# A hybrid attention and gating layer on eight cores: normalizing out of PSUM before the gate, and a wider tie rule in the planner

## What is computed

```python
h = rmsnorm(x, norm_g)
proj = einsum('bsd,de->bse', h, w_in) + b_in               # 1024 -> 2816
q, k, v, z_a, u_s, v_s, z_s = split(proj)                  # 512,128,128,512,512,512,512
attn = banded_sink_attention(q, k, v, sinks) * silu(z_a)   # window 128, 8 heads, 2 kv heads
#   probs = exp(scores) / (sum(exp(scores)) + exp(sink)) in effect, then probs @ v
sgu = chunked_spatial_gating(gelu(u_s), gelu(v_s), ...) * silu(z_s)
x = x + einsum('bse,ed->bsd', concat([attn, sgu]), w_out) + b_out
return rmsnorm(x, final_norm_g)
```

## Time and profile before

| what | value |
| --- | --- |
| median of 3 runs | 537.83 us (537.43 to 538.85) |
| profiled execution, its own time | 538.59 us |
| its span on the slowest core (core 3) | 537.0 us |
| spans of the other cores | 531.6 to 536.5 us |
| mean granted TensorE clock, the cores | 0.984 to 0.990 |
| TensorE matmul busy | 491.4 us, 91% |
| VectorE / ScalarE / GpSimd busy | 301.6 / 319.4 / 220.8 us |

### The profile page before, as it was taken

One profiled execution on the slowest core, in us unless ns is written; L12 is line 12 of the kernel. 1 busy time (PEld: TensorE's weight loads), 2 busy tenths in 40 slices (PEclk: granted clock), 3 DMA queues, 4 the chain that ended last, 5 costly groups with the idle time before them and its releaser, 6 DMA issues.

```text
span 537.0 us, 10160 instructions; the slowest of 8 cores (531.6 to 537.0 us)
## 1 busy us (share of the span) xinstructions
PE 491.4 (91%) x3422; PEld 234.5 (44%) x3422; DVE 301.6 (56%) x434; ACT 319.4 (59%) x543; POOL 220.8 (41%) x271
## 2 busy tenths in 40 slices
PE   1899999779999999999999999999999999997983
PEld 1346444334444445444454445444544445442431
DVE  2866865444374564455655556465565456675444
ACT  4336875563677674867558474957478545367422
POOL 2001686345045515361445515471356745432501
PEclk9999999898999999999999999999999999998998
DMA  8999993940031381472234713390344013311003
GB/s 237 337 344 319 331 213 53 204 175 1 1 118 41 76 264 54 157 163 74 112 125 135 180 41 138 138 234 2 123 153 103 17 60 139 117 79 79 2 22 136
DMA packets 43971, 71.11 MB, mean 132 GB/s; under 512 B 27536, under 2 KB 27664, under 8 KB 43920
## 3 DMA queue, kind: packets, MB, share of 16 engines
q1 hardware_dynamic: 42624, 68.32, 41.1%
q0 software_dynamic: 1152, 2.10, 2.5%
q10 hardware_dynamic: 144, 0.05, 0.0%
HBM read 49.48 MB, written 16.78 MB: 123 GB/s over the span
## 4 chain that ended last, share of the span: by engine, by line
PE 72%; DVE 8%; POOL 6%; issue 6%; DMA 5%; ACT 2%; SPq 0%; POOLq 0%; DVEq 0%; ACTq 0%
PE pp L516 36%; PE pp L776 18%; PE pp L580 8%; DMA LR<-sgu_wT 3%; PE pp L704 3%; PE pp L541 2%; PE pp L713 2%; POOL xe L760 2%; DMA xa<-x 2%; POOL uT L632 2%; PE pp L661 2%; DVE w_fm L462 1%; DVE mixT L638 1%; POOL xa L760 1%; DVE w_vs L462 1%
## 5 line engine op out<-in xcount | busy, mean ns | idle before, releaser
L516 PE MATMUL pp<-xT,w_fm 128*128 128x512 bf16 x1088 | 250.7, 387 | 6.6 <-DVE xn L730 3.6
L516 PEld LDWEIGHTS pp<-xT,w_fm 128*128 128x128 bf16 x1088 | 105.5, 99 | 138.1 <-issue 21.7
L776 PE MATMUL pp<-w_out_bf,mixT 128*128 128x512 bf16 x512 | 119.4, 381 | 2.4 <-DVE mixT L747 1.9
L760 POOL TENSOR_TENSOR xe<-xe,bout_sb 128x1024 f32<-128x1024 f32 x28 | 65.7, 2351 | 31.2 <-DVE xe L790 17.7
L776 PEld LDWEIGHTS pp<-w_out_bf,mixT 128*128 128x128 bf16 x512 | 47.6, 98 | 60.9 <-issue 7.4
L735 POOL TENSOR_TENSOR LR<-LR,zaT 128x512 f32<-128x512 f32 x28 | 32.4, 1156 | 80.0 <-DVE PT L691 64.4
L723 ACT ACTIVATE LR<-pp,esink 128x128 f32<-128x128 f32 x128 | 36.4, 366 | 38.4 <-PE pp L713 38.2
L781 DVE TENSOR_TENSOR xe<-pp,xe 128x512 f32<-128x512 f32 x56 | 38.3, 687 | 28.7 <-PE pp L776 28.2
L580 PE MATMUL pp<-w_vs,xT 128*128 128x512 bf16 x224 | 51.2, 379 | 0.4 <-DVE v_r L549 0.4
L688 ACT ACTIVATE PT<-pp 128x1536 bf16<-128x1536 f32 x31 | 45.1, 1455 | 1.9 <-PE pp L668 1.9
L526 ACT ACTIVATE zaT<-pp,pack_a_sb 128x512 bf16<-128x512 f32 x32 | 21.8, 686 | 40.9 <-PE pp L516 40.9
(11 more groups left out here) (79 smaller groups left out, 552.2 us busy)
## 6 DMA issues: line engine op xcount, KB each, us to landing
xa<-x SPq DMA_DIRECT2D x32, 512.0 KB, 6.2
xe<-x SPq DMA_DIRECT2D x28, 512.0 KB, 3.3
out<-xe SPq DMA_DIRECT2D x28, 512.0 KB, 2.7
xe<-w_in SPq DMA_DIRECT2D x12, 512.0 KB, 11.7
mixT<-w_in SPq DMA_DIRECT2D x10, 512.0 KB, 14.4
w_out_bf<-w_out POOLq DMA_DIRECT2D x8, 256.0 KB, 11.7
out<-xa SPq DMA_DIRECT2D x4, 512.0 KB, 2.7
LR<-sgu_wT SPq DMA_DIRECT2D x1, 512.0 KB, 16.5
```

Source lines behind the costliest of these rows:

```text
L516: ins = e.matmul(bank(h), lhsT=w_fm[:, FM.index(cb), k, :], rhs=xT[:, xb, k, :], start=(k == 0), stop=(k == 7))
L760: fn = lambda e: e.tensor_tensor(out=r[:, s, :], in0=r[:, s, :], in1=bout[:], op=ALU.add)
L776: ins = e.matmul(bank(h), lhsT=mixT[:, mb, ec, tt * 128:(tt + 1) * 128], rhs=w_out[:, ec, hf * 512:(hf + 1) * 512], start=(ec == 0), stop= ...
```

## The change

The two multiplies at the end of an attention tile change places, in all stages but the last, where nothing changes. VectorE multiplies the weighted values in PSUM by LR and writes the product into LR; then GpSimd multiplies LR by the gate and writes mixT. The bank pair's last reader is now the VectorE multiply right behind ScalarE's exponential. The second part replaces the planner's tie width of 0.02 us by 0.2 us, for every engine and every pick. Costs, priorities and the number of operations stay.

```diff
+TIE = 0.2
...
-                    if eb is None or key[0] < eb[0][0] - 0.02 or (key[0] < eb[0][0] + 0.02 and key[1:] < eb[0][1:]):
+                    if eb is None or key[0] < eb[0][0] - TIE or (key[0] < eb[0][0] + TIE and key[1:] < eb[0][1:]):
...
-            G.op("pool", lambda e: e.tensor_tensor(out=LR[:, lb, :].rearrange("p (c q) -> p c q", c=4),
+            G.op("dve", lambda e: e.tensor_tensor(out=LR[:, lb, :].rearrange("p (c h q) -> p c h q", c=4, h=2),
+                                                  in0=banks(V)[:, :, 0:256].rearrange("p h (c q) -> p c h q", c=4),
+                                                  in1=LR[:, lb, :].rearrange("p (c h q) -> p c h q", c=4, h=2), op=ALU.mult),
+                 uses=[V], writes=[("LR", lb)], cost=0.69, prio=v0 - 0.6)
+            G.op("pool", lambda e: e.tensor_tensor(out=mixT[:, mb, 0:4, j * 128:(j + 1) * 128],
                                                    in0=LR[:, lb, :].rearrange("p (c q) -> p c q", c=4),
                                                    in1=zaT[:, :, j * 128:(j + 1) * 128], op=ALU.mult),
-                 reads=[("LR", lb)] + [("zaT", c) for c in range(4)], writes=[("LR", lb)], cost=1.15, prio=v0 - 0.5)
-            G.op("dve", lambda e: e.tensor_tensor(out=mixT[:, mb, 0:4, j * 128:(j + 1) * 128].rearrange("p c (h q) -> p c h q", h=2),
-                                                  in0=banks(V)[:, :, 0:256].rearrange("p h (c q) -> p c h q", c=4),
-                                                  in1=LR[:, lb, :].rearrange("p (c h q) -> p c h q", c=4, h=2), op=ALU.mult),
-                 uses=[V], reads=[("LR", lb)], writes=[("mixA", mb, j), ("mst", 2 * mb), ("mst", 2 * mb + 1)], cost=0.69, prio=v0 - 0.6)
+                 reads=[("LR", lb)] + [("zaT", c) for c in range(4)],
+                 writes=[("mixA", mb, j), ("mst", 2 * mb), ("mst", 2 * mb + 1)], cost=1.15, prio=v0 - 0.5)
```

## The result

The changed kernel takes 524.59 us (median), the kernel before 538.12 us beside it: ratio 0.9744, 95% interval [0.9722, 0.9767].

The account below looks back on a forecast made before the run. TensorE bounds the kernel, with a matmul in flight 491.4 of 537.0 us. -3.4 (90 to 104 us) - 2.8 (435 to 490 us) - 0 (middle stages) + 1.0 (tie width) = -5.2 us gave 532.6 us, range 527.0 to 540.5.

Parts of the forecast that it names:

- durations: Both multiplies at an attention tile's end keep their times: 28 x (-0.005) = -0.1 us on VectorE, 0 on GpSimd.
- hidden GpSimd multiply: At the tile's end the GpSimd multiply is covered, its reader running a stage later; uncovered it would cost 1.16 us a tile.
- the harmless turn with the mask: VectorE's mask multiply must take turns with GpSimd, up to 1.16 us, but the mask usually waits for ScalarE anyway.
- Rival 1: Both bank-wait places close fully and middle stages lose their idle: 12.5 us gain, 525.4, or 526.4 with tie cost; chance 0.16.
- Rival 2: Banks come free but nothing follows, through mask turns or other VectorE work ahead of the multiply: 537.6 us; chance 0.13.
- place A: 90 to 104 us: three bank waits of 3.7 us can go, plus clock loss; 3.4 us taken, 4.95 at most.
- rival 3: Slower: the residual add goes ahead of the row statistics more often, 3.9 us each time; 541 us, chance 0.17.
- place B: 435 to 490 us, attention tiles of stages 6 and 7: idle and clock loss shrink; 2.8 us taken, 5.6 at most.
- The middle stages: Between 180 and 360 us TensorE is nearly full: 0 taken, with 1.9 us of idle in three stages as the end.
- The rule that was weighed: Middle stages: judged by MFU and weight-load busy time they would not be full and could hold more than 1.9 us.
- The tie rule: All queues: tie width 0.2 idles TensorE at 9 or 10 contested picks, 0.9 us; +1.0 us taken.

Follow-up runs that it names:

- run 2: The changed kernel with the old tie width 0.02, so the new dataflow alone, against the kernel before: 522.07 us, ratio 0.9693.
- Run 7: The kernel before, tie width 0.02, with the new dataflow in the four attention tiles of stage 6 alone: 528.13 us, ratio 0.9823.
- run 5: The kernel before, tie width 0.02, with the new dataflow in the four attention tiles of stage 0 alone: 533.62 us, ratio 0.9913.
- run 6: The kernel before, tie width 0.02, with the new dataflow in stages 1 to 5 alone: 534.86 us, ratio 0.9941.

## Why the prediction was wrong

**The mechanism was right, the sizes were not.** The release of the bank pair (theory R) is what pays; durations, hidden GpSimd multiply, the harmless turn with the mask: as forecast. Rival 1, at 0.16, comes nearest (526.4 with the tie cost, against 524.6), and even it falls short. Rival 2 did not happen as a whole, but its last clause, other work of VectorE ahead of the multiply, did in run 2, at place A. A stall of rival 3's kind, GpSimd's queue blocked ahead of the row statistics, came once, in the setup: 5.5 us of TensorE, behind a load and not behind L760; the gains outweigh it.

**The term that failed is place B**: "Ends 0 and 5.6; I take the middle, 2.8". Run 7, whose order is that of the kernel before up to stage 6, gives 9.5 us, above the upper end. (In the changed kernel the wide tie would have closed this place without the release, by the table above; the term is judged on the narrow one, on which its rows were read.) Two things were missed. First, how far the chain can be pulled up: the release itself was reckoned at 8.7 us at least, but then halved, because TensorE's work seemed to hold it. The end of ScalarE's exponential phase shows the truth. Before (its table loads at the ends of stage 0 and of stages 6 and 7, and the last output groups):

```profile
105.45 1.28 ACT L425 ACT_TABLE_LOAD   x1
...
487.35 1.28 ACT L425 ACT_TABLE_LOAD   x1
...
513.71 13.97 PE L776 MATMUL pp<-w_out_bf,mixT 128*128 128x512 bf16 x64 [1.94 <-DVE mixT L747]
```

Run 7:

```profile
474.23 1.28 ACT L426 ACT_TABLE_LOAD   x1
...
496.70 20.88 PE L788 MATMUL pp<-w_out_bf,mixT 128*128 128x512 bf16 x96
```

The phase ends at 474.23 and not at 487.35, 13.1 us earlier, of which some 2 us are an earlier start of that core. From its first table load to this one the phase takes 62.2 us before and 51.1 in run 7, on all eight cores: 11.1 us shorter. TensorE's work did not hold it: output groups were put off. Second, what becomes of them: 96 matmuls of L788 (12 groups) now stand behind the last projection, where 64 (8 groups) stood. They run while the last gate multiplies finish, so the wait of 1.94 us ahead of them is gone; I had counted only the two gaps before the phase's end. From 430 us on TensorE idled 1.07 + 0.84 + 3.59 + 0.36 + 1.94 = 7.8 us before and 2.0 us in run 7: 5.8 us. The clock, 487 to 513 us, before and run 7:

```profile
487.00:513.00 26.00, 23.88 (x128) 10.65 (x128) 12.66 (x24) 13.51 (x21) 9.85 (x14) 0.93 0.06 21
```

```profile
487.00:513.00 26.00, 26.00 (x122) 11.73 (x121) 13.33 (x19) 8.02 (x13) 6.23 (x9) 1.00 0.08 32
```

At 0.93, 26 us lose 1.8 us; I had 1.2. With 5.8 that is 7.6 us of the 9.5. The rest shows on the other cores: from the end of the phase to the last matmul the lower clock cost 1.7 to 3.4 us before, median 3.0, and nothing in run 7. Core 3 is among the lowest; on core 5 the wait of 1.98 us before L776 was followed by a clock of 0.66 from 514 to 517 us. On the median core the whole stretch falls from 11.7 to 2.3 us, 9.4 of the 9.5.

**Place A had about the right size for a wrong reason.** "The three waits of 3.7 us can go whole", 3.4 us taken; run 5 gives 4.7, of which lost time in stage 0 is 3.1 (8.3 to 5.2) and 1.4 lies at the end, where what the clock costs differs between cores. But the long wait did not go. Timeline of run 2 at that place:

```profile
91.61 0.63 ACT L728 ACTIVATE LR<-LR 128x512 f32<-128x512 f32 x1
...
93.29 0.75 DVE L483 TENSOR_SCALAR xn<-xa,st_rs 128x1024 bf16<-128x1024 f32 x1 [1.87 <-POOL st_rs L477]
...
93.96 0.68 DVE L736 TENSOR_TENSOR LR<-pp,LR 128x512 f32<-128x512 f32 x1
...
94.89 0.30 PE L705 MATMUL pp<-PT,v_r 128*64 128x256 bf16 x2 [2.47 <-DVE LR L736]
...
97.86 1.28 ACT L426 ACT_TABLE_LOAD   x1
```

L705 still waits 2.47 us, and the clock of 90 to 120 is 0.94 in runs 2 and 5. Here the exponential is done at 92.24, but VectorE has the scaling of xn (L483) ahead of the multiply in its queue, and that waits for GpSimd's row factor. That an earlier release is possible does not put the multiply at the head of the queue. (In the changed kernel the order differs and this wait is absent.) The gain came from the phase again: the table load that ends it is at 97.86, not 105.45, so the Gelu groups start earlier, the row statistics (GpSimd, 101.78 to 107.48) are not behind a late add, and the wait of the earlier trace rows, 2.73 us there and 1.9 on the average core, is gone. The prediction had used that chain as a reason to take 1.5 us off.

**The middle stages**: "0 taken", with 1.9 us of idle in three stages as the end; run 6 gives 3.2 us in five. Only about 1 us of it lies there: lost time in stages 1 to 5 falls from 2.8 to 1.8 us on the median core, as in the table above. Another 1.6 us are at the end (11.7 to 10.1), and 0.5 in stage 0, whose order run 6 does not touch and where the wait for the row statistics differs between cores by more than that (0.5 to 2.9 us before). So the busy rows did bound these stages. The rule that was weighed there (the Trainium skill, page "Perfetto Trace Analysis", section "Identifying the Most-Contended Engine") judges headroom by MFU and weight-load busy time. Weight loads are busy for less than half of each stretch, which read that way would be tens of us in each; the runs found about 1 us in five stages, and TensorE's best stretch here is 59.64 us of 60. None of the runs looked for more by other means.

**The tie rule**: +1.0 taken, 2.7 to 2.9 measured with the new dataflow, and -1.7 with the old one. The sign depends on the graph it meets, and by the table it is a balance of places that gain and places that lose. So a price from contested picks, the same for either, was the wrong kind of estimate.

By terms: forecast -3.4 - 2.8 - 0 + 1.0 = -5.2; runs -4.7 - 9.5 - 3.2 + 2.9 = -14.5, measured as a whole -13.5. The forecast and its range failed because I capped place B at the gaps and clock loss that its rows named and then took half, and held rival 1 for a corner case, though the shortened holds (8.7 us at least) exceeded the gap of 4.4 that they were set against.

## What to carry to other kernels

When a scarce buffer is held by a chain of engines, put the read that frees it directly behind its last input, and move everything that doesn't need the buffer behind that read, even if the chain as a whole gets no shorter. Price it by the phase or the serial chain that the buffer paces, and not by the waits that name it: here those were 7.3 us (3.7 and 3.6), and the gain 16.5. And try a planner's parameter apart from the change it comes with: without the wider tie this kernel is another 0.5% faster. Where its own effect looks like nothing, look by stage: here it hid a gain and a loss of some 10 us each. All of this is one kernel and one planner.

## What was not expected of the hardware

GpSimd's stall before its first load of w_out: 3.4 to 5.3 us in the five kernels in which the load comes ahead of the last statistics of stage 0, at most 1.7 us where those stand ahead of it. The load starts at 64.3 to 68.6 us in the former and 61.5 to 67.9 in the latter. So it looks like a wait for something that arrives and not a cost of the instruction. The DMA engines were all but fully busy then (share 1.00 in 60 to 71.4 us). The traces point to GpSimd's own instructions: on all eight cores of all 14 traces an 8 KB packet on an instruction queue (queue 14 on the page) ends 0.9 to 1.6 us before this load starts. On core 6 of the changed kernel GpSimd's operation before ends at 61.99, the packet at 65.65, and the load starts at 67.05. No run tested this, so it is not shown to be the cause.

After the 5.5 us gap behind this stall in the changed kernel the granted clock was 0.66 from 71.4 to 76 us; after gaps of 0.84 and 3.59 us it was 0.51, after 2.54 us 0.50.
